# Moving the state-space matrices' transposes and taps behind both products of a pair in a two-block decoder trunk

## What is computed

```python
for i in range(DEPTH):                      # DEPTH = 2
    x = x + 0.5 * swiglu(rmsnorm(x, ln_ffn1[i]), ffn1_w_in[i], ffn1_w_out[i])
    h = rmsnorm(x, ln_mix[i])
    out = hgrn2_mixer(h, ...) if i == 0 else s5_mixer(h, ...)
    x = x + out
    x = x + 0.5 * swiglu(rmsnorm(x, ln_ffn2[i]), ffn2_w_in[i], ffn2_w_out[i])
return rmsnorm(x, ln_final), states

# in s5_mixer, per group of 16 channels with 64 complex states:
lam_bar = exp(lam * dt)
b_bar = ((lam_bar - 1) / lam) * b
s[t] = lam_bar * s[t - 1] + b_bar @ u[t]    # a scan over time
y = real(c @ s) + d_skip * u
```

## Time and profile before

| | before |
|---|---|
| median of 3 runs | 2488.98 us (2487.93 to 2489.5) |
| profiled execution, its own time | 2480.59 us |
| its span | 2478.8 us |
| PE busy | 2337.1 us (94%) |
| DVE busy | 1220.8 us (49%) |
| ACT busy | 701.8 us (28%) |
| mean granted TensorE clock | 0.975 |
| DMA | 211.08 MB, 85 GB/s |

### The profile page before, as it was taken

One profiled execution on the slowest core, in us unless ns is written; L12 is line 12 of the kernel. 1 busy time (PEld: TensorE's weight loads), 2 busy tenths in 40 slices (PEclk: granted clock), 3 DMA queues, 4 the chain that ended last, 5 costly groups with the idle time before them and its releaser, 6 DMA issues.

```text
span 2478.8 us, 42614 instructions
## 1 busy us (share of the span) xinstructions
PE 2337.1 (94%) x17438; PEld 2294.5 (93%) x17438; DVE 1220.8 (49%) x1730; ACT 701.8 (28%) x878; POOL 2.7 (0%) x15
## 2 busy tenths in 40 slices
PE   6999999899999979999999999999955999999998
PEld 6999999889999879999999999999945999999998
DVE  5755544756667665432344443243377434433333
ACT  3222222334434333221222322122234432221223
POOL 0000000000000000000000000000000000000000
PEclk9999999999999999999999999999967999999999
DMA  4223432432231115323422332322333233223322
GB/s 125 82 65 109 122 85 64 121 108 70 73 84 52 44 53 135 96 69 93 113 80 85 89 85 64 105 69 66 87 107 102 74 85 86 80 73 84 85 70 70
DMA packets 398495, 211.08 MB, mean 85 GB/s; under 512 B 23025, under 2 KB 393922, under 8 KB 398402
## 3 DMA queue, kind: packets, MB, share of 16 engines
q1 hardware_dynamic: 387666, 198.03, 28.8%
q10 hardware_dynamic: 10736, 11.77, 1.5%
HBM read 193.01 MB, written 20.94 MB: 86 GB/s over the span
## 4 chain that ended last, share of the span: by engine, by line
PE 87%; DVE 7%; issue 2%; ACT 2%; DMA 0%; ACTq 0%; SPq 0%; DVEq 0%
PE ps L1687 78%; PE ps L1822 2%; PE ps L1657 2%; DVE rstd L1045 1%; PE ps L1857 1%; PE ps L1871 1%; PE ps L1986 1%; PE ps L1987 1%; DVE w_lo L1024 0%; ACT w_hi L657 0%; PE ps L1878 0%; PE ps L1765 0%; DVE sq L1547 0%; PE ps L1864 0%; DVE sq L1550 0%
## 5 line engine op out<-in xcount | busy, mean ns | idle before, releaser
L1687 PE MATMUL ps<-h_hi,w_hi 128*128 128x288 f32 x3328 | 723.4, 299 | 14.5 <-DVE t_a L1050 11.6
L1687 PE MATMUL ps<-h_hi,w_lo 128*128 128x288 f32 x3328 | 713.9, 296 | 0.0
L1687 PE MATMUL ps<-h_lo,w_hi 128*128 128x288 f32 x3328 | 713.5, 296 | 0.0
L1687 PEld LDWEIGHTS ps<-h_hi,w_hi 128*128 128x128 f32 x3328 | 536.6, 189 | 20.2 <-issue 6.5
L1687 PEld LDWEIGHTS ps<-h_hi,w_lo 128*128 128x128 f32 x3328 | 537.4, 189 | 0.0
L1687 PEld LDWEIGHTS ps<-h_lo,w_hi 128*128 128x128 f32 x3328 | 537.3, 189 | 0.0
L1024 DVE TENSOR_TENSOR w_lo<-w_raw,w_hi 128x2048 fp32r<-128x2048 f32 (+3 forms) x184 | 369.8, 2010 | 123.8 <-ACT w_hi L657 122.1
L657 ACT ACTIVATE w_hi<-w_raw 128x2048 fp32r<-128x2048 f32 (+3 forms) x184 | 309.5, 1682 | 216.8 <-PE ps L1687 204.6
L1687 PE MATMUL ps<-g_hi,w_hi 128*128 128x288 f32 x1408 | 304.7, 298 | 0.0
L1687 PE MATMUL ps<-g_lo,w_hi 128*128 128x288 f32 x1408 | 303.2, 297 | 0.0
L1687 PE MATMUL ps<-g_hi,w_lo 128*128 128x288 f32 x1408 | 303.0, 297 | 0.0
(11 more groups left out here) (301 smaller groups left out, 1860.5 us busy)
## 6 DMA issues: line engine op xcount, KB each, us to landing
w_raw<-in_ffn_w_in_dram SPq DMA_DIRECT2D x176, 512.0 KB, 4.8
w_raw<-in_ffn_w_out_dram SPq DMA_DIRECT2D x64, 384.0 KB, 3.7
w_raw<-in_ffn_w_out_dram SPq DMA_DIRECT2D x64, 320.0 KB, 3.4
w_raw<-in_hgrn_w_in_dram SPq DMA_DIRECT2D x32, 512.0 KB, 5.3
w_raw<-in_s_w_glu_dram SPq DMA_DIRECT2D x16, 512.0 KB, 4.7
wb_d<-wb_st ACTq DMA_DIRECT2D x8, 512.0 KB, 2.7
wc_d<-c_pow ACTq DMA_DIRECT2D x8, 512.0 KB, 3.5
s_in<-in_state_hgrn_dram SPq DMA_DIRECT2D x8, 512.0 KB, 3.9
```

The source lines that it names most:

```text
L1687: ins = M.matmul(ps[:, 2 * s + h, 0:HALF], w[j][:, at:at + P], v[:, k, h * HALF:(h + 1) * HALF], start=k == 0 and n == 0, stop=k == ph.kt ...
```

## The change

On PE, `b_turned` goes from between a pair's two products to behind the second, ahead of `taps`. On ACT, the copies to `wb_st` and their DMA go from `unit(i, 0)` to the end of `unit(i, 1)`. On DVE, `c_part` goes from `unit(i, 0)` to `unit(i, 1)`, behind the low part of the next weights. And `powers()` is cut in three, placed in three successive gaps between tiles of the first up phase.

```diff
@@ act, ffn_down, unit, j == 0
                             nc.scalar.activation(o[STATE:P], v[STATE:P, :, 1], ACT.Copy).then_inc(ct_done, 1)
-                            act.wait_ge(bl_full, ct + 1)
-                            act.wait_ge(wb_st_done, ct * 16)
-                            for q in range(2):
-                                ins = nc.scalar.activation(wb_st[:, q].rearrange("p s q -> p (s q)"), ps[:, 4 + q, :],
-                                                           ACT.Copy)
-                            ins.then_inc(wbst_done, 1)
-                            act.wait_ge(wbst_done, ct + 1)
-                            act.wait_ge(begun, 1)
-                            act.dma_start(wb_d[ct], wb_st[:]).then_inc(wb_st_done, 16)
@@ act, ffn_down, unit, behind norm_tile
                     if pieces and j == 1:
+                        act.wait_ge(bl_full, ct + 1)
+                        act.wait_ge(wb_st_done, ct * 16)
+                        for q in range(2):
+                            ins = nc.scalar.activation(wb_st[:, q].rearrange("p s q -> p (s q)"), ps[:, 4 + q, :],
+                                                       ACT.Copy)
+                        ins.then_inc(wbst_done, 1)
+                        act.wait_ge(wbst_done, ct + 1)
+                        act.wait_ge(begun, 1)
+                        act.dma_start(wb_d[ct], wb_st[:]).then_inc(wb_st_done, 16)
                         act.wait_ge(tap_full, ct + 1)
                         act.wait_ge(kz_st_done, ct * 32)
@@ dve, powers
-                for n in (1, 2, 4):
+                double_powers((1, 2))
+
+            def double_powers(counts):
+
+                for n in counts:
...
+            def last_powers():
+
+                double_powers((4,))
                 for q in range(2):
                     link(V.tensor_copy(lam_r[:, q], lam_p[:, q, :, 0:LIFT][:, :, ::-1]))
...
+            def long_powers():
 
                 link(V.tensor_copy(row(12), lam_p[:, 0, :, LIFT]))
@@ dve, ffn_up
                     powers()
                     unit(3, 1)
-                    first = 4
-                with dve.Fori(first, ph.pairs - 1) as i:
-                    for j in range(2):
-                        unit(i, j)
+                    last_powers()
+                    unit(4, 0)
+                    long_powers()
+                    unit(4, 1)
+                    first = 5
+                if first < ph.pairs - 1:
+                    with dve.Fori(first, ph.pairs - 1) as i:
+                        for j in range(2):
+                            unit(i, j)
@@ dve, down, unit
                     if pieces and j == 0:
                         b_part(i + ph.name[1] * (NK // 2))
+                    if pieces and j == 1:
                         c_part(i + ph.name[1] * (NK // 2))
@@ pe, down, pair_of
                         product(ph, 0, 0, i, hi, lo, first)
+                    product(ph, 1, 0, i, hi, lo, None, (HEADS - 1, HEADS) if begun_at else None)
                     if pieces:
                         b_turned(i + ct0)
-                    product(ph, 1, 0, i, hi, lo, None, (HEADS - 1, HEADS) if begun_at else None)
-                    if pieces:
                         taps(i + ct0)
```

## The result

| | before | after |
|---|---|---|
| median | 2489.24 us (2487.93 to 2491.3, 4 runs) | 2472.29 us (2469.45 to 2474.59, 4 runs) |
| profiled execution, its own time | 2480.59 us | 2471.5 us |
| its span | 2478.8 us | 2469.8 us |
| PE / DVE / ACT busy | 2337.1 / 1220.8 / 701.8 us | 2334.7 / 1219.6 / 702.4 us |
| mean granted clock | 0.975 | 0.976 |

The ratio is 0.9931, 95% interval 0.9916 to 0.9945. That is 17 us faster (14 to 21), where 11.6 were forecast; 2472.3 lies inside the range of 2468 to 2485.

What follows compares the result with a forecast made beforehand. PE was taken to bound the kernel (87% of the chain), the DVE-ACT round the second down phase; -6.6 - 7.4 + 2.4 = -11.6 us from a median of 2489.0 gave 2477.4 us, range 2468 to 2485.

Steps and rivals of the forecast that it cites:

- `powers()` in three: First up phase: PE's 4.9 us stall behind `powers()` goes, plus 1.7 us of low clock behind it: -6.6 us.
- First down phase: All four PE waits at `b_turned` go and none arises at `taps`: -7.4 us, bounds 0 and -7.4.
- Second down phase: DVE-ACT round grows from 23.9 to 25.4 us, PE's wait moves before `taps`: mixer starts 1.9 us later, +2.4 with clock.
- The mixer's start: Clock term: the mixer's first matmuls run partly at the lower clock, +0.5 us, as taps take up part of that stretch.
- The last rival: Longer idle time keeps the clock low through the second down phase: +40 us, 2517 us; chance 0.05.
- The forecast's last step: Whole kernel: -11.6 us applied to the median, 2489.0, since the profiled execution was 8.4 us shorter: 2477.4 us.
- the forecast with its bounds: Whole kernel: the main forecast of 2477.4 us, lying between 2475 and 2482 us; chance 0.62.
- second rival: The second down phase does not get longer, `wb_st` copies finding a gap: -14 to -18, about 2473 us; chance 0.14.
- Every wait simply goes: First rival: all waits at `b_turned` in both down phases vanish: -33, 2456 us; chance 0.06.
- The second phase not longer: Second rival: copies to `wb_st` find a gap in the second down phase: about 2473 us; chance 0.14.
- the wait moves to `taps`: Third rival: the first down phase's wait only moves to `taps`: -4.2, 2484.8 us; chance 0.13.
- slower: Last rival: clock stays low through the second down phase, four pairs make +40, 2517 us; chance 0.05.

Runs made afterwards that it cites:

- e2: Kernel before with only `powers()` cut in three, down phases in the old order: 2482.77 us, ratio 0.997 to before.
- e9: Kernel before, unedited, timed and profiled once more: 2488.79 us, ratio 1.0001.
- e3: Kernel after with `powers()` whole again, so only the order in the two down phases is changed: 2482.07 us, ratio 0.997 to before.
- e6: Kernel before with four extra ACT copies ahead of those to `wb_st`, in `unit(i, 0)`: 2489.11 us, ratio 1.0002.
- e1: Kernel after, unedited, timed once more against before: 2473.76 us, ratio 0.9938.
- e5: Kernel after with four extra ACT copies ahead of those to `wb_st`: 2474.42 us, ratio 0.9944 to before.
- e8: e7 plus the mixer's waits for `wbst_done` and `kz_done` placed later on PE: 2459.81 us, ratio 0.9884 to before.
- e4: Kernel after with the second down phase in the order of before: 2470.3 us, ratio 0.992 to before.
- e12: e8 plus an earlier ACT split of the next pair's first weight tile, its low part on DVE before `h_lo`: 2456.65 us, ratio 0.9863 to before.
- e7: Kernel after with ACT splitting the next pair's second weight tile before the `wb_st` and `kz` copies and DMAs: 2464.91 us, ratio 0.9893 to before.

## Why the prediction was right, and by how much its terms were off

**`powers()` in three: right, low clock undersized.** The wait of 4.9 us went as predicted, and the clock reads 1.00 through the stretch. The term was -6.6, given as its own bound; e2's profile has the first up phase at 148.08 against 155.60 in e9, -7.5. The difference lies in the 1.7 us put down to the lower clock: that came from one execution, and in e3 and e9 the same 384 matmuls took 53.91 and 53.76 us, not 52.84, so 2.7 to 2.8 us over the full rate.

**First down phase: right, and more.** All four waits went, none came at `taps`, and the margin of 1.5 us before `taps` measured 1.4. The term was -7.4, again with nothing below it; e3 against e9 gives 217.25 - 226.94 = -9.7. Two things were priced at nothing. Behind a 2 us wait the clock sometimes falls, 1.5 us in one of four pairs in each of three executions (e2, e6, e9). And eight transposes that follow a running product add 0.88 us to PE's chain where those behind a wait add 1.09, four times 0.2.

**Second down phase: the mechanism right, the new round right, the old one only in part.** Predicted were rounds of 25.4 us; 25.4 and 25.1 came, with `wb_st` directly behind `sq`. The mixer's first matmul came 22.0 us after the last of these low parts (506.76 - 484.76; predicted 22.2), and the stage grew by 1.9 us (100.42 against 98.53 in e1 and e9; the forecast had +1.9 by the same working). Between the two profiles first shown it is only +1.4 (100.38 - 98.94). "Nothing in that round waits for PE" holds for the round of 23.9 us that the prediction read. The next one, 25.08 us, has 1.30 us of DVE waiting for PE, and before the change such waits stood in three or all four pairs of each of the two profiles. The change took them out while it put the copies in, so the two rounds grew by 0.6 us together and not by 1.5 each: 25.40 and 25.14 in e1 against 24.54 and 25.45 in e9. The other 1.3 us between these two profiles came in the first pair (0.5, where the forecast had -0.9) and behind the last low part (0.8, forecast 1.0). So the +1.9 is right in sum, and partly by chance in its pieces. e5 to e8 show that it is this queue and no other cause: longer copies lengthen the round in after and not in before, and taking them out of the way gives 22 us rounds. That PE's wait would move before `taps` "some 6 us in one piece" was too long: the four are 3.95, 3.95, 4.59 and 3.12 us. The taps behind them, at the lower clock in part, take 2.6 to 3.6 us instead of 1.9, which fills most of the rest.

**The mixer's start: undersized.** The clock term was +0.5. It is the step where the prediction said that the taps take up part of the low stretch. They did, and were not enough: between the waits of 3.12 and 1.72 us PE does only 2.61 us of taps, and the first seven pairs of the mixer's matmuls come 0.48 to 0.62 us apart instead of 0.27. PE's timeline of the kernel after, beside the earlier trace rows:

```profile
502.44 2.61 PE L1781 MATMUL ps<-c_pow,b_blk 128*32 128x128 f32 x16 [3.12 <-DVE c_pow L1236]
506.76 0.82 PE L1703 MATMUL ps<-h_hi,w_hi 128*128 128x288 f32 x2 [1.72 <-issue]
```

From there to `rstd` it takes 9.2 to 9.6 us instead of 7.6, so the term was +1.6 to +2.0. In e3, with the very same order of instructions there, it took 7.59: the clock fell for the taps (0.54 from 510.6 to 514.0 us) but was back before the mixer's first matmul (1.00 from 514.9 to 518.0). Of the four profiles with this order (after, e1, e3, e5) three have the term, 1.6 to 2.0 us, and one has not.

**The clock in the second down phase.** Behind the second of the four waits for `c_pow` the clock fell for the taps and was back before the product, by the windows' rows:

```profile
452.20:455.70 3.50, 3.46 (x16) 2.62 (x16) 2.07 (x3) 2.35 (x4) 0.00 (x0) 0.52 0.52 150
456.00:460.00 4.00, 4.00 (x32) 4.00 (x31) 0.38 (x1) 2.26 (x4) 0.00 (x0) 1.00 0.49 162
```

The 16 taps took 3.56 us there (452.24 to 455.80) instead of 1.94, and as the round has time to spare, that cost nothing. By the Trainium skill, "TensorE: Matmul & The Clock Gate", "HAM oscillation", a kernel that idles in each tile starts each at the lower clock; the trace agrees: granted clocks of 0.66, 0.52, 0.50 and 0.72 over the taps of the four pairs. The last rival, a clock low through the whole phase, did not come (0.92 over the phase).

**The sum.** With the terms of typical executions: -7.5 - 9.7 + 1.9 + 1.8 = -13.5 us instead of -11.6. The medians differ by 17.0 in the first comparison and 15.8 in e1's; the interval of the latter (-12 to -19 us) holds -13.5, that of the former (-14 to -21) just misses it. The 2 to 3 us between are not settled: the rest of the span, which the change does not touch, reads 1959.9 to 1968.7 over all profiles, and its clock differs from one execution to the next, so one profile a kernel can't say whether that part gained. The forecast's last step, from the profiled execution to the median, was right in direction: that execution lies 8.4 us low, and e9's profile minus it shows where: 1.4 and 1.5 us in the two stages ahead of the second down phase and 4.6 in the rest (-0.4 in the second down phase). But those 2.9 us lie just where the change relieves PE, and the terms read from the low profile did not have them to give.

**How much of the hit is luck.** The path and the signs of all terms came as predicted. The number did not: 2472.3 lies below the 2475 to 2482 that the prediction gave to the forecast with its bounds, and near the 2473 of its second rival, which the stages refute. It lies inside the stated range because that range had room for this rival. And an undersized loss (1.3 us at the mixer) hid part of two undersized gains (0.9 and 2.3).

**The rivals.** *Every wait simply goes* (-33) fell: the waits at `b_turned` in the second phase set its pace only in small part, by the 0.5 to 2.4 us that DVE waited for product 1 behind them. *The second phase not longer* fell by e4 and by the three profiles of the new order at 100.4 us, *the wait moves to `taps`* by the first down phase's missing waits, *slower* by the medians. e12 comes to the -33 us of the first rival, but by emptying the DVE-ACT round, not by moving PE's wait.

## What to carry to other kernels

When PE waits in every repetition, add up the round of the engines it waits for before you count the wait as gain: here a wait of 14 us moved (to `taps`, to the low parts, to the mixer) and shrank only when ACT's queue had the split ahead of the copies (15.6 us to 9.8 in e7) and DVE's the low part ahead of `h_lo` (6.2 in e12). Put into an engine's queue first what another engine waits for, and copies out and their DMA issues behind it. And take low-clock terms from several executions: one profile had none of the 1.5 us losses that three others showed.

## What was not expected of the hardware

- A wait of 2.1 us was enough, in some executions, to bring the granted clock down in the product behind it (in e9 0.69 to 0.73 over the 6 us from 208 on, and 11.1 us instead of 9.58 for 72 matmuls), and in others with the same wait not.
- Eight transposes of 128x128 add 0.88 us to PE's chain directly behind a product and 1.09 behind a wait, all at the full clock. In the timeline they last 1.03 us in the first case, and begin 0.16 us before the product's end.
- Executions of one kernel differ by 3 to 10 us, while the first three stages of the kernel after repeat within 0.04 us in its two profiles.
